# Attention of a fused hybrid block: values as the stationary operand, both row tiles of a head as moving columns, two heads per pass in the two column halves of the array, and probabilities normalised before they are transposed

## The reference, cut to what matters

```python
def blk(qi):                                     # 128 query rows at a time
    s = jnp.einsum('bqhgd,bkhd->bhgqk', qi, k) * 64 ** -0.5
    p = jax.nn.softmax(s, axis=-1)
    return jnp.einsum('bhgqk,bkhd->bqhgd', p, v)
...
def step(S, inp):                                # gated delta rule, 4 heads, chunks of 64 tokens
    v_new = u_i - w_i @ S
    o = (q_i * exp(g_i)) @ S + qk_i @ v_new
    S = S * exp(g_last) + (k_i * exp(g_last - g_i)).T @ v_new
...
cat = concatenate([fourier, o_att, dn], axis=-1) # 256 + 512 + 256 channels
return cat @ w_out
```

## Time and profile before

| what | us |
|---|---|
| median of the runs (lowest to highest) | 1581.68 (1578.07 to 1581.94) |
| the profiled execution | 1582.5 |
| its span, first to last instruction | 1580.7 |
| TensorE busy in the span | 1473.7 (93%) |
| VectorE busy | 873.5 (55%) |
| ScalarE busy | 693.4 (44%) |

### The profile page before, as it was taken

How to read it: one execution, slowest core, us unless ns; L and a number is a source line. 1 busy time by engine, 2 the same in 40 slices (tenths; PEclk the granted TensorE clock), 3 DMA queues, 4 the chain that set the end, 5 groups by cost and what they waited for, 6 DMA issues and landing times. The chain is left out here.

```text
span 1580.7 us, 27212 instructions
## 1 busy us (share of the span) xinstructions
PE 1473.7 (93%) x11365; PEld 1239.4 (78%) x11365; DVE 873.5 (55%) x1366; ACT 693.4 (44%) x1162; POOL 59.2 (4%) x73
## 2 busy tenths in 40 slices
PE   3899989988999989999899999999999989999996
PEld 1556777655999969898777999978989887799985
DVE  0564342435555555567686545475547768554555
ACT  3132225433444434476742444453447653344442
POOL 0000450000000000000000000000000000000000
PEclk9999999998999989999999999999999999999998
DMA  9521553005545317432336555523633223845420
GB/s 354 214 86 54 182 197 107 1 1 190 179 164 211 117 51 213 160 108 92 123 107 234 194 190 207 186 78 122 181 107 119 97 106 107 305 174 212 172 93 27
DMA packets 120897, 230.17 MB, mean 146 GB/s; under 512 B 20065, under 2 KB 34529, under 8 KB 120033
## 3 DMA queue, kind: packets, MB, share of 16 engines
q1 hardware_dynamic: 117776, 221.37, 40.4%
q10 hardware_dynamic: 3024, 7.44, 1.3%
HBM read 227.76 MB, written 1.05 MB: 145 GB/s over the span
## 5 line engine op out<-in xcount | busy, mean ns | idle before, releaser
L741 DVE TENSOR_TENSOR work_rounded<-ring,work_rounded 128x1024 fp32r<-128x1024 f32 x208 | 240.9, 1221 | 102.6 <-ACT work_rounded L733 102.4
L704 PE MATMUL psum<-channels_rounded,work_rounded 128*128 128x256 f32 x2048 | 286.9, 287 | 0.0
L704 PEld LDWEIGHTS psum<-channels_rounded,work_rounded 128*128 128x128 f32 x2048 | 272.7, 196 | 3.9 <-issue 2.5
L715 PE MATMUL psum<-work_rounded 128*128 128x512 f32 x1152 | 265.7, 390 | 0.0
L733 ACT ACTIVATE work_rounded<-ring 128x1024 fp32r<-128x1024 f32 x208 | 203.2, 1050 | 122.2 <-PE psum L715 118.5
L957 PE MATMUL psum<-channels_rounded,ring_rounded 128*128 128x256 f32 x1728 | 250.4, 286 | 2.7 <-PEq L2816 1.5
L715 PEld LDWEIGHTS psum<-work_rounded 128*128 128x128 f32 x1152 | 214.7, 188 | 43.6
L957 PEld LDWEIGHTS psum<-channels_rounded,ring_rounded 128*128 128x128 f32 x1728 | 224.1, 192 | 9.5 <-issue 8.7
L1425 DVE TENSOR_TENSOR ring_rounded<-ring,ring_rounded 128x1024 fp32r<-128x1024 f32 x80 | 94.2, 1198 | 48.9 <-ACT ring_rounded L1229 48.4
L781 DVE TENSOR_TENSOR work<-work 128x512 f32<-128x512 f32 x48 | 33.2, 692 | 109.8 <-ACT work L753 109.8
L753 ACT ACTIVATE work<-psum 128x512 f32<-128x512 f32 x48 | 28.7, 598 | 140.5 <-PE psum L704 140.5
(11 more groups left out here) (364 smaller groups left out, 1979.3 us busy)
## 6 DMA issues: line engine op xcount, KB each, us to landing
ring<-in_w_in SPq DMA_DIRECT2D x20, 2048.0 KB, 8.0
ring<-in_w_ff SPq DMA_DIRECT2D x16, 2048.0 KB, 8.0
ring<-in_w_ff_in SPq DMA_DIRECT2D x16, 2048.0 KB, 8.4
ring<-in_w_ff_out SPq DMA_DIRECT2D x16, 2048.0 KB, 7.9
ring<-in_w_mod SPq DMA_DIRECT2D x12, 2048.0 KB, 9.2
ring<-in_w_out SPq DMA_DIRECT2D x6, 2048.0 KB, 8.7
ring<-in_w_in SPq DMA_DIRECT2D x8, 1024.0 KB, 5.8
ring<-in_w_up SPq DMA_DIRECT2D x4, 2048.0 KB, 7.9
```

What stands on the lines that cost most here:

```text
L704: mm = pe.matmul(psum[:, 4 + 2 * half + q, i * SEQ:(i + 1) * SEQ], w1[pw][:, k, m * P:(m + 1) * P], y[py][:, k, :], start=((k, n) == (0, 0 ...
L715: mm = pe.matmul(psum[:, 2 * t + n, :], h[ph][:, kq, t * P:(t + 1) * P], w2[pw][:, kq, n * 512:(n + 1) * 512], start=False, stop=False, sk ...
L741: dve.tensor_tensor(parts.low[i % 2][:, at], ring[:, SLOT * s + 1024 * c:SLOT * s + 1024 * (c + 1)], exact(parts.high[i % 2][:, at]), ALU. ...
```

## The change

The second product of the attention is turned round. The values (128 keys x 64 channels) are the weights, and both row tiles of a head, 256 queries, are the moving columns. The result comes channel-major, 64 channels x 256 queries, so two heads fill one bank: head 2p in partitions 0 to 63, head 2p + 1 in partitions 64 to 127. There are 4 such jobs `PV{p}`, each of 8 products (16 MATMULs), where there were 16 of 4; ScalarE copies each to its place in `catT3` (128x256), and `catA0`, `catA1` and the 16 scaled reads of line 2418 are gone. `pt` becomes two buffers of 128 x 4 x 256, one for each head of a pair.

A channel-major result can't be scaled by query with a value per partition. So `share(i)` on VectorE now computes the reciprocal, waits for it, and multiplies `pr[i % 2]` (128x512) by it, and TensorE's transposes of `PT{i}` wait for that (`probs_scaled`), where they waited for the exponential.

The order of the queues changes with it. Scores run two items ahead where they ran one ahead: `S0` and `S1` stand in front of the loop, and ScalarE makes both exponentials there.

```diff
-                    def values(i):
-                        ps = w.open(f"PV{i}")
-                        w.after(f"PT{i}")
+                    def values(p):
+                        ps = w.open(f"PV{p}")
+                        w.after(f"PT{4 * p + 3}")
+                        c0 = P + HD * (p // 2)
                         for k in range(4):
-                            c0 = P + HD * (i // 8)
-                            mm = pe.matmul(ps[:, 0:HD], pt[i % 2][:, k * P:(k + 1) * P], akv3[:, k, c0:c0 + HD],
-                                           start=(k == 0), stop=(k == 3))
+                            for hh in range(2):
+                                mm = pe.matmul(ps[half(hh), 0:SEQ], akv3[:, k, c0:c0 + HD], pt[hh][:, k, :],
+                                               start=(k == 0), stop=(k == 3))
                         w.done(mm)
...
                     def probs_T(i):
...
-                        w.after(f"S{i}")
+                        pe.wait_ge(probs_scaled, i + 1)
...
                     for n in range(8):
...
+                        if n in (2, 4, 6):
+                            values(n // 2 - 1)
                         probs_T(2 * n)
-                        scores(2 * n + 1)
+                        if n < 7:
+                            scores(2 * n + 2)
...
-                        values(2 * n)
                         probs_T(2 * n + 1)
                         if n < 7:
-                            scores(2 * n + 2)
-                        values(2 * n + 1)
+                            scores(2 * n + 3)
+                    values(3)
...
                     def share(i):
                         r.after(f"S{i}")
-                        dve.reciprocal(rden[:, i:i + 1], den[:, i:i + 1]).then_inc(rden_ready, 1)
+                        do(dve.reciprocal(rden[:, i:i + 1], den[:, i:i + 1]))
+                        dve.tensor_scalar(pr[i % 2], pr[i % 2], rden[:, i:i + 1], None, ALU.mult).then_inc(probs_scaled, 1)
...
-                        maximum(2 * n + 1)
                         share(2 * n)
+                        if n < 7:
+                            maximum(2 * n + 2)
...
+                        share(2 * n + 1)
                         if n < 7:
-                            maximum(2 * n + 2)
-                        share(2 * n + 1)
+                            maximum(2 * n + 3)
```

More of the change, by code:

```diff
@@ L239, in first_jobs @@
     for n, t in enumerate(TILES_D):
-        if n == 2:
-            j.add("S0", "act", wide=True)
+        if n >= 2:
+            j.add(f"S{n - 2}", "act", wide=True)
         add("act", f"U{t}", f"W{t}")
@@ L245, in first_jobs @@
             j.add(f"WS{n}", "dve", wide=True)
-        add("act", f"PT{2 * n}", f"S{2 * n + 1}")
+        if n in (2, 4, 6):
+            j.add(f"PV{n // 2 - 1}", "act", wide=True)
+        add("act", f"PT{2 * n}")
+        if n < 7:
+            add("act", f"S{2 * n + 2}")
         j.add(f"SU{n}", "dve", wide=True)
@@ L249, in first_jobs @@
             add("dve", f"QS{n}", f"AV{n}")
-        add("act", f"PV{2 * n}", f"PT{2 * n + 1}")
+        add("act", f"PT{2 * n + 1}")
         if n < 7:
-            j.add(f"S{2 * n + 2}", "act", wide=True)
-        j.add(f"PV{2 * n + 1}", "act", wide=True)
-    for n in ("catA0", "catA1", "catD", "g0_0", "g0_1", "g1_0", "g1_1"):
+            add("act", f"S{2 * n + 3}")
+    add("act", "PV3")
+    for n in ("catD", "g0_0", "g0_1", "g1_0", "g1_1"):
         j.add(n, "act")
@@ L1750, in first_block @@
             tmp, gate_tmp = over(4096, 1024), [over(5120, 512), over(5632, 512)]
-            f_tok, f_mid = over(6144, 512), catT[:, 1024:2048]
+            f_tok, f_mid = over(6144, 512), catT[:, 512:1536]
             kv_tok, dkT = v3(over(0, 2048), 512), v3(over(2048, 1024), 512)
             k_squares, q_squares = over(3072, 1024), over(4096, 512)
-            dqT = v3(catT[:, 512:1024], 256)
+            dqT = v3(catT[:, 1536:2048], 256)
             gate_rows = over(6656, 512)
@@ L2109, in _ @@
                     for n, t in enumerate(TILES_D):
-                        if n == 2:
+                        if n >= 2:
                             w.after("akT")
-                            scores(0)
+                            scores(n - 2)
                         ps = w.open(f"U{t}")
@@ L2413, in probs, with probs_T @@
                                                        scale=0.125, accum_out=den[:, i:i + 1]))
-                    def values(i):
+                    def probs_T(i):
                         h, t = i // 2, i % 2
-                        act.wait_ge(rden_ready, i + 1)
-                        r.read(f"PV{i}", act.mul(aq3[:, t, h * HD:(h + 1) * HD], r.open(f"PV{i}", HD), rden[:, i:i + 1]))
+                        ps = r.open(f"PT{i}")
+                        if h >= 2:
+                            act.wait_ge(products_done, j1.full(f"PV{h // 2 - 1}"))
+                        r.read(f"PT{i}", act.activation(pt[h % 2][:, :, t * P:(t + 1) * P], v3(ps, P), ACT.Copy))
                     for n, t in enumerate(TILES_D):
-                        if n == 2:
-                            probs(0)
+                        if n >= 2:
+                            probs(n - 2)
                         ps = r.open(f"U{t}")
@@ L2430, in _ @@
                     for n in range(8):
[L2431 to L2434, removed]
+                        if n in (2, 4, 6):
+                            copy(f"PV{n // 2 - 1}", catT3[:, 1 + n // 2, :], SEQ)
+                        probs_T(2 * n)
                         if n < 7:
                             probs(2 * n + 2)
-                        values(2 * n + 1)
-                    copy("catA0", catT[:, 512:1024])
-                    copy("catA1", catT[:, 1024:1536])
+                        probs_T(2 * n + 1)
+                        if n < 7:
+                            probs(2 * n + 3)
+                    copy("PV3", catT3[:, 5, :], SEQ)
                     copy("catD", catT[:, 1536:2048])
@@ L2726, in share @@
                         r.after(f"S{i}")
-                        dve.reciprocal(rden[:, i:i + 1], den[:, i:i + 1]).then_inc(rden_ready, 1)
+                        do(dve.reciprocal(rden[:, i:i + 1], den[:, i:i + 1]))
+                        dve.tensor_scalar(pr[i % 2], pr[i % 2], rden[:, i:i + 1], None, ALU.mult).then_inc(probs_scaled, 1)
                     maximum(0)
+                    maximum(1)
                     r.after("U1")
```

8 lines of the change are left out of this document (5 added, 3 removed).

## The result

The changed kernel takes 1612.6 us (median of 4 runs, 1609.7 to 1616.5), the kernel before 1581.8: a ratio of 1.0202, 95% interval 1.0173 to 1.0231. The change makes the kernel 31 us slower. Slower was forecast, 8 us of it. The profiled execution took 1609.7, its span is 1607.9, 27.2 more than before.

What follows compares the result with a forecast made beforehand. TensorE was taken to bound the loop, with VectorE following; after the change they would take turns. Loop 5.45, front 1.7 and behind 0.7 gave + 7.9 us on the span of 1580.7, forecast 1590.0, range 1582 to 1599.

Steps and rivals of the forecast that it cites:

- The loop's sum: Steps 1 to 6, `WS1` to `WS7`: engines taking turns make 52.44 us against 46.99, + 5.45.
- `WS7` to `catD` + 0.7: Behind the loop: step 7's chain on VectorE starts at about 6.1 us after `WS7` instead of 5.38, + 0.7.
- The part in front of the loop: Before `WS1`: a second exponential delays `W1`'s copy and VectorE's first shares, + 1.7 us, lower bound 0.
- The gain of the turned product: On TensorE: two old products per step, 2.08 us, give way to a turned one of 1.86, three inside the steps.
- the faster rival: In the loop: TensorE stays the bound if scaled probabilities are ready when `WS` ends; - 8.2 us, time 1573.5, chance 0.09.
- The clock falls in the loop: TensorE's clock drops to the lower level in some stretches of the loop; + 3 to + 10 us, 1593 to 1600, chance 0.15.
- The case that I chose: Whole kernel: TensorE and VectorE take turns; + 7.9 us, 1590.0, itself spanning 1585 to 1594, chance 0.60.
- that 3.2: TensorE's 3.2 us idle at the end of a stretch before the change, after which the clock is 0.58.
- one to three steps' worth: In the loop: how many steps' doubled TensorE time a clock fall costs, 5 us each at worst, partly hidden under VectorE.
- The drain at a change of mode: Around the three `PV` inside the loop: a drain of 0.2 us twice each would make the sum 9.1 instead of 7.9.
- the halves in turn: In each `PV`: column halves run one after the other, 3.44 us instead of 1.86; + 4.7, time 1594.7, chance 0.07.
- overlapping hand-overs: On VectorE: reciprocal and multiplication cost 0.35 us together instead of 0.68, twice per step; + 3.3, time 1585, chance 0.09.

Runs made afterwards that it cites:

- e2: Changed kernel with VectorE's queue reordered, each item's reciprocal and multiplication ahead of what TensorE delivers late: 1575.5 us, ratio 0.9956 to the kernel before.
- e3: Changed kernel without the multiplication of the probabilities, so the attention's result is not normalised: 1571.5 us, ratio 0.9925 to the kernel before.
- e1: Changed kernel with wide filler products in TensorE's waits in front of the transposes: 1592.8 us, ratio 1.0057 to the kernel before.
- e7: Changed kernel with the old product in place of the turned one and e2's order of VectorE: 1579.6 us, ratio 0.9977 to the kernel before.
- e5: e4 with more filler products in step 0 and none after step 1: 1615.8 us, ratio 1.0199 to the kernel before.
- e8: e2 without filler products in the loop and with the gate products moved in front of `catD`: 1568.7 us, ratio 0.9897 to the kernel before.
- e10: Kernel before without its four filler products: median 1596.7 us; of ten runs five took 1579.3 to 1582.5 and five 1611.0 to 1619.0.
- e6: Changed kernel with more filler products for items 0 and 1, the rest as it was: 1606.2 us, ratio 1.0148 to the kernel before.
- e4: Changed kernel's order and multiplication, but with the old product, one in each of TensorE's two waits per step: 1623.2 us, ratio 1.0239 to the kernel before.
- e11: e1 with its filler made of identity transposes in place of wide products: 1589.6 us, ratio 1.0041 to the kernel before.

## Why the prediction was wrong

Forecast were 1590.0 us, in a range from 1582 to 1599; measured were 1612.6.

- The bound before, and its change: right. TensorE set the pace, and behind the change it waits for VectorE twice per step, in the two places named, released by the multiplication. e2 shows that the cause is VectorE's order, e3 that the multiplication itself is free.
- The loop's sum: right to 0.02 us in 52.4, once the clock is held (e1), with no step off by more than 0.04. The multiplication took 0.487, as taken; a `PV` 1.88, taken as 1.86; so the halves run beside each other. `WS7` to `catD` + 0.7, as forecast. The part in front of the loop + 2.0, forecast + 1.7. In e1 the stretch grew by 8.4, forecast 7.9. (The last line of the sum gives 1590.4 less 0.8, which is 1589.6, as 1590.0; nothing hangs on it.)
- The gain of the turned product: it was said to be worth nothing in the changed kernel, and is worth 4 to 5 us where TensorE is the bound (e7 against e2). The time of the faster rival, 1573.5, is nearly that of e2 (1575.5), whose queue meets the condition that the rival named; its loop shrank by 6.2, where the rival had 6.9.
- What failed is the clock: the rival "The clock falls in the loop" with its chance of 0.15 and its price of + 3 to + 10. The case that I chose has it at 1.00 throughout. Two steps of that working were wrong. The first: "waits of 1.3 and 1.6 us, none as long as that 3.2". I took the longest idle time in front of a known fall as what a fall needs; in the changed kernel it fell behind a single wait of 1.6 in step 0, in e5 behind waits of 0.25 and 0.59, and in e8 behind next to none. The second: "one to three steps' worth". I priced a fall as passing; the lower level lasted for 82 us in all, since the loop's work wins the upper one back only now and then. Measured, this term is 23.6 us, where the rest of the change is 8.4. I also put the filler at a cost alone ("would cost what they cost now" if the waits were gone); without it e8 lost the clock in step 1, and half of the runs of e10 took 30 us more.
- The drain at a change of mode, the halves in turn, overlapping hand-overs: none occurred.

What stays open: what exactly in the work makes TensorE's clock fall or return. The runs show cases, not the criterion: it fell with TensorE busy 7.72 of 8.00 us by the profile's row (e8), was kept through waits of 0.35 and 0.69 between filler (e6) and not through 0.25 and 0.59 without (e5), came back once in e4 with no turned product near, and was held in e11 by transposes. Every clock in the table is that of one profiled execution per kernel, and e10 shows that runs of one kernel can differ.

## What to carry to other kernels

Where a stage of small products holds the upper clock, treat that as a resource that the stage may be near to losing: before a change puts a wait on TensorE, price the whole stage at the lower clock, not only the wait, and look for filler that stands there already. When an operation moves to an engine with a strict queue, compute what stands ahead of it in that queue; moving it by one item, in front of what arrives late, was worth 37 us here, most of it through the clock, while the operation itself cost nothing. Where times of one kernel fall into two groups with two mean clocks, three runs can miss one of them, as the first three of e10 did: compare the clocks before the medians.

## What the runs showed of the hardware that was not expected

- TensorE's lower clock outlasts its cause: in e4 it stayed at 0.50 for 54 us in which TensorE was busy 53.
- Waits of 0.25 and 0.59 us in a step of 8.9 us went ahead of its loss (e5), and in e8 next to none, with TensorE busy 7.72 of the 8.00 us in front of the fall.
- 28 filler products where the changed kernel had 4, all in waits, took 20 us off the launch (e1).
- Forecast, and now with rows of its own: two products of 64 weight columns in the two halves run beside each other. 16 MATMULs of 256 columns take 1.88 us at the upper clock, where the prediction's sum for halves in turn was 3.44, and 3.6 at the lower (315.73 to 319.34).
